# Sums of squares of four norms: two matmuls on a high and a low part in place of one in single precision

## The reference

```
def _rms_norm(x, g):
    xf = x.astype(jnp.float32)
    y = xf * lax.rsqrt(jnp.mean(xf * xf, axis=-1, keepdims=True) + RMS_EPS)
    return (y * g.astype(jnp.float32)).astype(x.dtype)

for layer in range(2):
    h = _rms_norm(x, norm_mix_pre[layer]);  m = mixer(h)
    x = x + _rms_norm(m, norm_mix_post[layer])
    h = _rms_norm(x, norm_ffn_pre[layer]);  f = _conv_ffn(h)
    x = x + _rms_norm(f, norm_ffn_post[layer])
# then, once:
x = x + gated_deltanet(rms_norm(x, norm_mix_2))
x = x + squared_relu_mlp(rms_norm(x, norm_mlp_2))
return rms_norm(x, norm_final_2)
```

## Time and profile before

| | |
|---|---|
| Runs of the kernel before | 1935.88 us median of 3 (1934.05 to 1936.56) |
| Profiled execution: span, from first to last instruction | 1933.6 us, 30753 instructions |
| Profiled execution, around the span | not given apart; the median of the runs lies 2.3 us above the span |
| PE busy (matmuls) | 1914.8 us, 99% |
| DVE busy | 1156.5 us, 60% |
| ACT busy | 818.0 us, 42% |
| Granted clock of PE | 1.000 over the span |
| Read from memory | 163.78 MB, 86 GB/s over the span |

### The profile page before, as it was taken

How to read it: one execution, slowest core, us unless ns; L and a number is a source line. 1 busy time by engine, 2 the same in 40 slices (tenths; PEclk the granted TensorE clock), 3 DMA queues, 4 the chain that set the end, 5 groups by cost and what they waited for, 6 DMA issues and landing times.

```text
span 1933.6 us, 30753 instructions
## 1 busy us (share of the span) xinstructions
PE 1914.8 (99%) x12210; PEld 1567.9 (81%) x12210; DVE 1156.5 (60%) x1891; ACT 818.0 (42%) x1327; POOL 27.4 (1%) x31
## 2 busy tenths in 40 slices
PE   9999999999999999999999999999999999999998
PEld 7777788888888877788888888877888778888887
DVE  6556577533655766657652555789988666425532
ACT  5457554333334454445332333465555543212232
POOL 0111000000000000000000000000000000000000
PEclk9999999999999999999999999999999999999999
DMA  6222123223223211131223222322111132322321
GB/s 222 77 77 77 49 83 107 78 98 109 89 88 128 71 45 66 66 109 66 87 87 109 104 83 82 112 67 79 56 62 46 66 109 87 109 87 88 108 87 66
DMA packets 30804, 168.61 MB, mean 87 GB/s; under 512 B 6456, under 2 KB 6616, under 8 KB 14816
## 3 DMA queue, kind: packets, MB, share of 16 engines
q1 hardware_dynamic: 25872, 161.69, 24.2%
q10 hardware_dynamic: 4816, 5.29, 0.9%
HBM read 163.78 MB, written 2.13 MB: 86 GB/s over the span
## 4 chain that ended last, share of the span: by engine, by line
PE 85%; DVE 8%; ACT 4%; issue 2%; DMA 1%; SPq 0%; DVEq 0%; ACTq 0%
PE bank L523 25%; PE bank L525 24%; PE bank L524 24%; PE bank L806 1%; ACT hH L1378 1%; PE bank L1172 1%; DVE hL L2194 1%; PE bank L989 1%; ACT wH L1378 1%; PE bank L818 1%; DVE x L2190 1%; PE bank L829 1%; PE bank L1013 1%; DVE wL L2117 1%; PE bank L1263 1%
## 5 line engine op out<-in xcount | busy, mean ns | idle before, releaser
L523 PE MATMUL bank<-hH,wH 128*128 128x512 f32 x1368 | 550.0, 402 | 1.8 <-DVE hL L2156 1.4
L525 PE MATMUL bank<-hH,wL 128*128 128x512 f32 x1368 | 532.1, 389 | 0.0
L524 PE MATMUL bank<-hL,wH 128*128 128x512 f32 x1368 | 531.4, 388 | 0.0
L1378 ACT ACTIVATE wH<-raw 128x2048 fp32r<-128x2048 f32 (+3 forms) x199 | 294.1, 1489 | 120.0 <-PE bank L525 104.8
L523 PEld LDWEIGHTS bank<-hH,wH 128*128 128x128 f32 x1368 | 257.2, 188 | 61.4 <-issue 9.1
L525 PEld LDWEIGHTS bank<-hH,wL 128*128 128x128 f32 x1368 | 256.8, 188 | 54.7
L2108 DVE TENSOR_TENSOR wL<-raw,wH 128x2048 fp32r<-128x2048 f32 x96 | 219.7, 2289 | 134.6 <-ACT wH L1378 134.6
L524 PEld LDWEIGHTS bank<-hL,wH 128*128 128x128 f32 x1368 | 257.5, 188 | 47.6 <-issue 1.2
L523 PE MATMUL bank<-mH,wH 128*128 128x512 f32 (+1 forms) x610 | 232.8, 382 | 0.0
L525 PE MATMUL bank<-mH,wL 128*128 128x512 f32 (+1 forms) x610 | 232.6, 381 | 0.0
L524 PE MATMUL bank<-mL,wH 128*128 128x512 f32 (+1 forms) x610 | 232.6, 381 | 0.0
(11 more groups left out here) (355 smaller groups left out, 2724.5 us busy)
## 6 DMA issues: line engine op xcount, KB each, us to landing
raw<-in_ffn_up SPq DMA_DIRECT2D x44, 1024.0 KB, 4.9
raw<-in_mlp_up SPq DMA_DIRECT2D x16, 1024.0 KB, 4.9
raw<-in_mlp_down SPq DMA_DIRECT2D x16, 1024.0 KB, 4.9
raw<-in_ffn_down SPq DMA_DIRECT2D x16, 768.0 KB, 4.3
raw<-in_odd_in SPq DMA_DIRECT2D x12, 1024.0 KB, 4.9
raw<-in_dn_qkv SPq DMA_DIRECT2D x12, 1024.0 KB, 5.0
raw<-in_ffn_down SPq DMA_DIRECT2D x16, 640.0 KB, 3.9
raw<-in_even_in SPq DMA_DIRECT2D x7, 1024.0 KB, 4.9
```

Of the source, the lines that this page charges most:

```text
L523: mm(out, a, c, start=first, stop=False, skip_group_check=joined)
L524: mm(out, a, d, start=False, stop=False, skip_group_check=joined)
L525: return mm(out, b, c, start=False, stop=last, skip_group_check=joined)
L1378: return nc.scalar.activation(out, in_, func, **kw)
```

## The change

For the four norms in `wide_sums`, `ss` is split like the projections' operands. ACT copies it into `sumH` in format float32r (in `root`, ahead of the wait for the sum), DVE subtracts, `ss - sumH`, into `sumL` (in `inverse_kept`), and PE multiplies a matrix of ones in that format, `onesR`, by the one and the other and accumulates both in bank 6. PE waits for the event of `sumL` in place of that of `ss`. `onesR` is copied once by ACT near the start. `sumH` and `sumL` lie over `sq`.

```diff
--- before.py
+++ after.py
@@ -186,6 +186,8 @@
         ss = sb("ss", [P, SEQ])
         dg = sb("dg", [P, TT, P])
         small = sb("small", [P, 64])
+        onesR = sb("onesR", [P, P], F32R)
+        sumH, sumL = sb("sumH", [P, SEQ], F32R, sq_at), sb("sumL", [P, SEQ], F32R, sq_at + 4 * SEQ)
         stat = sb("stat", [P, 64])
         base = place[0]
         ident, ones, window = const[:, 0:P], const[:, P:2 * P], const[:, 2 * P:]
@@ -661,10 +663,12 @@
 
             def token_sums(tag, event, i=None):
 
+                if tag in wide_sums:
+                    pe.wait_ge(*at(f"{tag}.sums_low"))
+                    mm(bank[6][:], onesR[:], sumH[:], start=True, stop=False)
+                    mm(bank[6][:], onesR[:], sumL[:], start=False, stop=True).then_inc(*tick("sums_pe", f"{tag}.sum{KT - 1}"))
+                    return
                 pe.wait_ge(*at(event, i))
-                if tag in wide_sums:
-                    mm(bank[6][:], ones, ss[:], start=True, stop=True).then_inc(*tick("sums_pe", f"{tag}.sum{KT - 1}"))
-                    return
                 for t in range(TT):
                     last = mm(bank[7][:, t:t + 1], ss[:, t * P:(t + 1) * P], ones[:, 0:1], start=True, stop=True)
                 last.then_inc(*tick("sums_pe", f"{tag}.sum{KT - 1}"))
@@ -1419,6 +1423,9 @@
 
             def root(tag):
 
+                if tag in wide_sums:
+                    act.wait_ge(*(at("dn_out.tile3.ss", looped("dn_out", 2) - 1) if tag == "mlp2" else at(f"{tag}.ss")))
+                    a(sumH[:], ss[:], ACT.Copy).then_inc(*tick("norm_act", f"{tag}.sums_high"))
                 act.wait_ge(*at(f"{tag}.sum{KT - 1}"))
                 if tag in wide_sums:
                     inverse_root(rinv, bank[6][:], DM, f"{tag}.log", f"{tag}.kept")
@@ -1632,6 +1639,7 @@
             input_norm()
             act.wait_ge(*at("in.const"))
             act.wait_ge(*at("in.vec"))
+            a(onesR[:], ones, ACT.Copy)
             act.dma_start(rope[:], dram["rope"]).then_inc(*tick("loaded_rope", "in.rope", 16))
 
             def gate_bias(g):
@@ -2134,6 +2142,9 @@
 
             def inverse_kept(tag, name):
 
+                if tag in wide_sums:
+                    dve.wait_ge(*at(f"{tag}.sums_high"))
+                    tt(sumL[:], ss[:], sumH[:].bitcast(F32), ALU.subtract).then_inc(*tick("norm_dve", f"{tag}.sums_low"))
                 if tag in ("mix_pre0", "mlp2"):
                     lo_early(name, 2)
                 if tag in wide_sums:
```

## The result

| | before | after | ratio after / before |
|---|---|---|---|
| median of 20 runs each | 1936.62 us (1934.05 to 1938.49) | 1939.57 us (1937.34 to 1941.58) | 1.0016, 95% interval 1.0010 to 1.0022 |
| span of the profiled execution | 1933.6 us | 1938.2 us | |

The change costs 2.95 us; 2.57 were forecast. The profiled spans lie 4.6 us apart, 1.7 us more than the runs.

A forecast was written before the change was run, and what follows sets the result against it. It took TensorE (PE), busy 1914.8 of 1933.6 us, to bound the kernel. Three places at +1.39 - 0.40 = +0.99 us and mlp2 at -0.40 gave +2.57, so 1935.88 + 2.57 = 1938.4 us, range 1935.4 to 1940.9 us.

The forecast's parts named there:

- The sum itself: At each of four places, two matmuls costing 0.46 us replace a single-precision sum costing 0.86: PE saves 0.40 us.
- The wait: At ffn_pre0, ffn_pre1 and mix2, PE waits 1.39 us longer for ACT's copy and DVE's subtraction, with nothing hiding it.
- mlp2: At this fourth place 2.0 us of slack makes the wait free; 0.40 us is gained, spacing 1.15 us.
- The sum +2.57 us: Over all four places: 3 x 0.99 - 0.40 = +2.57 us on a span of 1933.6 us.
- What stands behind the waits: Later projection matmuls, ACT's root and DVE's evictions lose no slack behind the longer waits: cost nothing.
- They move with PE: Behind the sum, root and evictions shift along: root about 0.9 us later, PE's stream 0.99 us later.
- the first matmul that needs an evicted bank: In unit 6 of the first up-projection; claimed far off, its tile evicted by 315.98, DVE caught up at 331.50.
- The clock stays at 1.00: PE's standstills of about 1.7 us at three places would not lower the granted clock; rival of a fall, 1965 us, chance 0.02.
- The span moves by what the four places add up to: Check on the changed profile: the forecast is wrong if the span moves by another amount than the four places' sum.
- 1938.4 us: Forecast time of the whole kernel: the earlier median 1935.88 us plus 2.57 us.

The follow-up runs named there:

- e1: Changed kernel without the split: PE waits for `ss` as before, the pair multiplies ones by ones, sums left out; 1934.96 us, ratio 0.9992.
- e2: Changed kernel with the old single-precision matmul on `ss`, still waiting for `sumL`; 1942.05 us, ratio 1.0027.
- e3: Changed kernel with the sums of ffn_pre0 and ffn_pre1 three steps later in PE's order; 1937.06 us, ratio 1.0006.
- e4: Kernel before with its single-precision sums of ffn_pre0 and ffn_pre1 three steps later; 1937.96 us, ratio 1.0005.
- c3: Changed kernel plus nine extra 128x512 matmuls in PE's idle time at 1296 us; 1938.29 us, ratio 1.0009.
- c1: e6 without PE's four waits for `onesR` and with nine extra 128x512 matmuls in PE's idle time at 1293 us; 1931.80 us, ratio 0.9976.
- e5: Kernel before, but DVE's last addition writes one rounded tile in the projections' format, summed by one matmul, no low part; 1935.83 us, ratio 1.0000.
- e6: e5 with the sums of ffn_pre0 and ffn_pre1 one step later in PE's order; 1935.58 us, ratio 0.9994.
- c2: e6 without PE's four waits for `onesR`, nothing else; 1935.54 us, ratio 0.9995.
- b2: The kernel before, unchanged, run once more for its profile; 1936.66 us.
- c4: The changed kernel, run once more for a second profile; 1939.63 us, ratio 1.0016.
- e7: Kernel before plus nine extra 128x512 matmuls into a free bank in PE's idle 2.1 us at 1293 us; 1935.47 us, ratio 0.9996.

## Why the prediction was right

- **The sum itself, -0.40 us.** Right: -0.43 at mlp2 and -0.37 behind a wait (e1). The pair costs two projection starts and 0.03 us of restart more than the old matmul had.
- **The wait, +1.39 us.** Right: 1.40 us by itself (e2), 1.54 - 0.15 of idle matmul unit in the changed kernel. The chain taken from the feed-forward's own split held to 0.02 us, since ACT and DVE stood idle at all three places, as the earlier trace rows said.
- **mlp2.** Right: no wait, 2.05 us of cover for the 2.0 forecast, 1.13 us for 1.15.
- **The sum +2.57 us.** The four places give +2.58 us. The runs say +2.95 (about 1.9 to 4.3 by the interval) and +3.10 us. The intervals would allow 2.58, but the traces have 0.54 us more in the two later waits, and 3.12 us is nearer to both. The start-ups of the profiles differ by up to 0.6 us in either direction, which hides this in a difference of two spans.
- **What stands behind the waits, "cost: nothing".** Wrong by 0.54 us. "They move with PE" held up to some 170 us behind mix2, and then two old waits of PE on ACT and DVE grew. In the feed-forwards the conclusion held, no new wait in the changed kernel, but one step of it was wrong. The prediction called "the first matmul that needs an evicted bank" far, by the evictions of the earlier trace rows, and took that for the nearest slack. The nearest is the weight split of unit 6 on DVE's queue, 1.27 us. That it did no harm has the reason that the prediction gave at mix2: root and PE moved by nearly the same amount. With ACT's root at 285.72, 0.77 us behind the pair's start where 0.7 was worked out, PE gained on DVE nothing that it could stumble over there. Moved by itself, the sum does stumble (e3, e4).
- **The clock stays at 1.00.** Right of the three waits that the change makes longer: in c3, with those three alone, no stretch is at 1.2 GHz. Wrong as a check on the profile: the changed kernel's clock does fall, behind the 2.1 us of idle that the earlier trace rows quoted as harmless. It was read from one execution, and that one lacked the fall: of ten later profiles without the nine matmuls each has one, and the three with them have none. At least 18 of the 88 runs of the kernel before lack it as well, by their mean clock.
- **"The span moves by what the four places add up to".** This failed: 4.6 for 2.58 us. By the traces: 0.30 start-up, 2.58 places, 1.5 clock, 0.54 the two later waits, and -0.3 spread over the rest.
- **1938.4 us.** 1.2 us low. 0.4 is the sum; the rest is the base, where 3 runs gave 1935.88 and 20 gave 1936.62. The 2.3 us between span and median could have warned: in every run on record the time lies 1.7 to 1.9 us above its own span, so the profiled execution, at about 1935.4 us, was faster than the median one.

## What to carry to other kernels

A cheaper matmul that needs its operand split gains two starts of four and pays the split's whole two-engine chain wherever the engine already waits for that operand; look at the wait in front of the instruction before its own price. Where a rounded sum will do, let the instruction that makes the tile write the format that is wanted, which has no chain; here that gained its 3.4 us only once PE's stop at 1454 us was gone (c1), and lost most of it otherwise (e5, e6, c2). A span from one profile is an anchor only with its clock stretches listed: one execution of the same program can lack a loss that ten other profiles have. A place-by-place spacing doesn't see the clock and agreed to 0.03 us in every profile here, but it sees the chosen places alone; laying the two instruction streams side by side found 0.54 us elsewhere.

## What the runs showed of the hardware

- **PE's clock fell to 1.2 GHz around 2.1 us of idle time** in b2, the changed kernel, c4 and the e-runs that kept this stretch, for 3.4 us mostly, 6.8 in c4. The stretch lies between small matmuls, 64 of 128x1 ahead of it and 64 of 32x32 behind. It fell around the 2.04 us of e6 and the 1.77 us of c2 too, not around the 1.52 us of e5, nor around the three waits of 1.52 to 1.54 us in any profile of the change. The cost is 1.5 us (aligned traces) for 3.4 us, and the start of it shifts from during the idle time (c4) to 1.6 us behind its end (e4). The Trainium skill ("TensorE: Matmul & The Clock Gate", Part 1) states that the number of matmuls at the lower clock when a kernel starts varies from run to run of one kernel; in the middle of this one the traces show such variation too, with one program (the kernel before) at 1.00 and at 0.51 over the same matmuls in two executions.
- **Nine useless matmuls cost next to nothing and save about 1.3 us** (e7 against the kernel before, 1935.47 and 1936.8 us; c3 against c4, 1938.29 and 1939.63), since PE would have idled for 2.1 of their 2.33 us; in e7's profile the small matmuls behind them start 0.08 us later than without them. The interval of e7's ratio has 1 in it; what speaks for the saving is that the two differences agree, and that it is near the 1.5 us that the fall costs in the aligned traces.
- **PE stops 1.5 to 2.0 us within an unrolled line of small matmuls** at 1454 us in e5, e6 and c2, with no semaphore behind it, and not in c1, before or after. In the transfer records of all fourteen profiles a block of instructions (16 KB, queue 8) is fetched near this place. In the eleven without a stop the transfer starts 2.1 to 2.7 us before the 64 small matmuls; in e5 and c2 it starts 0.2 us before them, in e6 0.4 us behind their start, and PE goes on 2.4, 2.7 and 2.4 us after the transfer began. So the stop fits a PE that waits for its own code. No run varied the transfer alone, and why it came late in these three is open. The Trainium skill ("Runtime: NRT & Kernel Launch", Instruction fetch mechanics) says that the cost of this fetch is mostly hidden where no branch is taken; if it is the fetch, these rows are an exception to that.
